# Unit 14's slots each fetched by two gathers with bounded row numbers

## The chip, the cores and the metric

The kernel runs on one core of a Trainium2 chip. The metric is the device time of one execution in microseconds. Before the change it is 949.93 us, the median of three runs (949.86 to 950.06). Engine names are those of the profile: PE is TensorE's matmul, PEld its weight load, DVE is VectorE, ACT ScalarE, POOL GpSimd, SP SyncE.

## What is computed

One layer of a hybrid decoder: windowed and block attention, cross-attention, and a product-key expert retrieval (PEER), for 256 tokens of width 1024 in float32. The change lies in the PEER part alone. It is, cut to its core:

```python
PEER_HEADS, PEER_N_KEYS, PEER_TOPK = 8, 128, 16
PEER_N_EXPERTS = PEER_N_KEYS * PEER_N_KEYS            # 16384 rows in each of u and v

def peer(h, w_q, sub_keys, u, v):
    ...
    sc = jnp.einsum('thpc,pkc->thpk', q, sub_keys)
    v1, i1 = lax.top_k(sc, PEER_TOPK)
    cand = (v1[:, :, 0, :, None] + v1[:, :, 1, None, :]).reshape(T, PEER_HEADS, PEER_TOPK * PEER_TOPK)
    cidx = (i1[:, :, 0, :, None] * PEER_N_KEYS + i1[:, :, 1, None, :]).reshape(...)
    top, pos = lax.top_k(cand, PEER_TOPK)
    experts = jnp.take_along_axis(cidx, pos, axis=-1).reshape(T, PEER_HEADS * PEER_TOPK)
    gates = jax.nn.softmax(top, axis=-1).reshape(T, PEER_HEADS * PEER_TOPK)
    ...
    a = jax.nn.gelu(jnp.einsum('cd,ced->ce', xc, u[ec]), approximate=False)
    y = jnp.einsum('ce,ced->cd', gc * a, v[ec])
```

Each token uses 8 heads x 16 experts, and each expert is a row of u (the dot product) and a row of v (what is added, weighted). The final RMSNorm follows.

## The kernel before

The host lays u and v side by side, so that expert e is one row of 2048 floats (8 KB) of `in_experts`, row numbers 0 to 16383.

**Units and slots.** A unit is one head of one tile of 128 tokens (one token on each partition); there are 16 (`UNITS`), numbered 0 to 15, the first eight for tokens 0 to 127. A unit has 16 slots (`TOPK`). Slot s of a unit is the s-th expert of each of its 128 tokens: 128 rows of 8 KB, 1 MiB, in one buffer of SBUF. There are 16 buffers (`BUFFERS`; their names in the trace are `arena` and `late_ring`), and from unit 5 on slot s always uses the same one, so a gather of slot s of a unit waits for the last use of slot s of the unit before.

**Who does what with a slot.** GpSimd issues its gather (`issue`, L2008): an indirect DMA that takes one row number for each partition from `expert[:, parity, s]`. When it has landed it adds 16 to the semaphore of the buffer, `slot_in[b]`. VectorE waits for this semaphore in `dot` (L1876) and computes the 128 dot products. For each pair of slots (`GROUP` = 2) ScalarE applies the gelu and the gates and writes two diagonal matrices (`weigh`, L1306 to L1321), and PE multiplies them with the v halves of the two rows (`use_pair`, L1020 and L1023, on quarters of the array; `use_group`, L957, in units 0 to 4 and 15) and adds up in PSUM. Its last matmul of a slot adds one to `slot_free`, for which GpSimd waits before it issues into the buffer again.

**The order on GpSimd.** Its queue is one list: units 0 to 4 written out, then `gather_unit` for unit 5, a loop over units 6 to 13, `gather_unit` for units 14 and 15. `gather_unit` waits for `experts_ready` once (the unit's row numbers, which VectorE computes two units ahead between its dot products and leaves in `expert`), and for each slot for `slot_free`. A wait is a wait and an empty instruction (`wait_apart`). The last two slots of unit 15 are fetched as u halves and v halves by four gathers (L2040) from `last_rows`.

**The end.** Unit 15's last eight slots go one by one (L1887, L1057); then VectorE and ScalarE normalise tile 1 and the result is stored.

The semaphore count that stands for the landing of slot (u, s) is `landed_count(u, s)`; it is used by `dot`.

Of the kernel before, what the change touches and what calls it, by code (L numbers as in the profile page):

```python
# [7 lines left out]
ALU = mybir.AluOpType  # L8
# [4 lines left out]
U32 = mybir.dt.uint32  # L13

P = 128
# [10 lines left out]
PEER_HEADS, PEER_KEYS, TOPK = 8, 128, 16  # L26
# [35 lines left out]
UNITS = TILES * PEER_HEADS  # L62
SLOTS = UNITS * TOPK
BUFFERS = 16
# [3 lines left out]
AHEAD = 2  # L68
SOFTMAX_AFTER = 6
QUERIES_FIRST = 3  # L70
GATES_AT_SLOT = 5


def over_slots(unit, first, last):
# [16 lines left out]
QUERY_UNITS = PEER_HEADS - QUERIES_FIRST  # L91
# [186 lines left out]
def build(nc, x_in, mem_in, rel_bias, panels, keys_in, experts, gain_cols, gain_rows, ident_in,  # L278
          onehot_in, mask_in, iota_in, out):
    with ExitStack() as ctx:  # L280
        def sb(name, shape, dt=F32):
            return ctx.enter_context(nc.sbuf_tensor(name, shape, dt))

        def sem(name):
            return ctx.enter_context(nc.semaphore(name))
# [24 lines left out]
        neg_max = sb("neg_max", [P, SOFTMAXES, TILES])  # L310
        row_max = sb("row_max", [P, SOFTMAXES, TILES])
# [23 lines left out]
        expert = sb("expert", [P, AHEAD, TOPK], U32)  # L335
# [7 lines left out]
        diag = sb("diag", [P, DIAGS, P])  # L343
        last_rows_f = sb("last_rows_f", [P, 2, HALVED])
        last_rows = sb("last_rows", [P, 2, HALVED], U32)


        with (nc.sbuf_tensor("arena_below", [P, 5120], F32),
# [45 lines left out]
        def at_buffer(b):  # L394

            return ring[:, b, :] if b < RING else late_ring[:, LATE[b - RING], :]

        def buffer_of(u, s):

            first = isinstance(u, int) and u < QUERY_UNITS  # L400
            return BUFFER_OF_SLOT[u * TOPK + s if first else ALL_FROM + s]

        def slot(u, s):

            return at_buffer(buffer_of(u, s))

        low_half, high_half = slice(0, P // 2), slice(P // 2, P)
        unused_raw = raw[:, (RAW_LOADED.index("qpeer4") + 1) % RAW_RING, :]
        crossed, nothing = unused_raw[:, 0:D], unused_raw[:, D:D + P]
        last_squares = slot(UNITS - 1, 0)[:, 0:D]  # L410
# [2 lines left out]
        def landed_count(u, s):  # L413

            if isinstance(u, int) and u < QUERY_UNITS:
                n = u * TOPK + s
                return 16 * BUFFER_OF_SLOT[:n + 1].count(BUFFER_OF_SLOT[n])
            before = BUFFER_OF_SLOT[:ALL_FROM].count(BUFFER_OF_SLOT[ALL_FROM + s])
            return u * 16 + 16 * (before - QUERY_UNITS + 1)

        def query_rows(h, t):

# [72 lines left out]
        experts_ready = sem("experts_ready")  # L495
# [3 lines left out]
        slot_in = [sem(f"slot_in{i}") for i in range(BUFFERS)]  # L499
        slot_free = sem("slot_free")  # L500
# [5 lines left out]
        crossed_out = sem("crossed_out")  # L506
        crossed_summed = sem("crossed_summed")
        last_rows_step = sem("last_rows_step")
        last_rows_ready = sem("last_rows_ready")
        last_down_in = [sem(f"last_down_in{i}") for i in range(HALVED)]  # L510
        last_dot = sem("last_dot")
# [37 lines left out]
        def wait_apart(eng, semaphore, value):  # L549

            eng.wait_ge(semaphore, value)
            eng.nop(nofuse=True)
# [896 lines left out]
        def _(dve):  # L1449
# [412 lines left out]
            def gate_weights(u):  # L1862

                dve.wait_ge(top_exp_ready, u + 1)
                nc.vector.reciprocal(top_inv[:], top_sum[:]).then_inc(gate_step, 1)
                dve.wait_ge(gate_step, u * 2 + 1)
                if not isinstance(u, int) or u:
                    dve.wait_ge(gate_taken, u)
                nc.vector.tensor_scalar(gate_next, top_exp[:], top_inv[:, 0:1], None, ALU.mult
                                        ).then_inc(gate_step, 1)  # L1870

            def dot(u, t, s):

                dve.wait_ge(slot_in[buffer_of(u, s)], landed_count(u, s))
                row = slot(u, s)[:, 0:D]
                i = nc.vector.tensor_tensor_reduce(row, row, h_rows[:, t, :], 1.0, 0.0, ALU.mult,  # L1876
                                                   ALU.add, dots[:, s:s + 1])
                if isinstance(u, int) and u == UNITS - 1 and s >= SINGLES_FROM:
                    i.then_inc(last_dot, 1)
                elif s % GROUP == GROUP - 1:  # L1880
                    i.then_inc(dots_ready, 1)
# [8 lines left out]
            def use_unit(u, t, routed=True):  # L1890

                for s in range(TOPK):
                    dot(u, t, s)
                    if s == GATES_AT_SLOT:
                        gate_weights(u + 1)
# [72 lines left out]
        def _(pool):  # L1968
# [38 lines left out]
            def issue(u, s, parity):  # L2007
                nc.gpsimd.indirect_dma_start(  # L2008
                    out=slot(u, s), out_offset=None, in_=experts,
                    in_offset=bass.IndirectOffsetOnAxis(ap=expert[:, parity, s:s + 1], axis=0),  # L2010
                ).then_inc(slot_in[buffer_of(u, s)], 16)
# [34 lines left out]
            def gather_unit(u, parity, joins=(), last=TOPK):  # L2046
                pool.wait_ge(experts_ready, u + 1)
                for s in range(last):
                    n = ALL_FROM + s
                    if n in joins:  # L2050
                        pool.wait_ge(product_ready, PLACE[f"qpeer{PEER_HEADS - 1}"] + 1)
                    elif joins and n < min(joins):
                        wait_apart(pool, slot_free, SLOT_BEFORE[n] + 1)
                    else:
                        wait_apart(pool, slot_free, u * TOPK + (s + 1 - BUFFERS))
                    issue(u, s, parity)

            gather_unit(QUERY_UNITS, QUERY_UNITS % AHEAD, [n for n in JOINS if n >= ALL_FROM])
            with pool.Fori(QUERY_UNITS + 1, UNITS - AHEAD, AHEAD) as u:
                for k in range(AHEAD):  # L2060
                    gather_unit(u + k, (QUERY_UNITS + 1 + k) % AHEAD)
            gather_unit(UNITS - 2, UNITS % AHEAD)
            gather_unit(UNITS - 1, (UNITS - 1) % AHEAD, last=TOPK - HALVED)
            pool.wait_ge(last_rows_ready, 1)
            for i in range(HALVED):
                s = TOPK - HALVED + i
# [100 lines left out]
```

## Time and profile before

| | us |
|---|---|
| median of three runs | 949.93 |
| the profiled execution | 950.31 |
| its span on the core | 948.5 |
| DVE busy | 621.1 |
| PE busy | 743.5 |
| POOL busy | 350.1 |
| gathers, issue to landing, median | 30.9 and 30.2 (two tiles) |

The span is what the profile of the program covers; the time of an execution has 1.8 us more around it. The profile divides the span into 40 slices of 23.7 us and gives the busy tenths of each engine in each; its DMA row is the mean busy share of the sixteen DMA engines, the row under it what they moved. The gathers of the experts begin at 292 us. The mean granted clock of TensorE is 0.903.

### The profile page before, as it was taken

What the parts mean: (1) busy time and instruction counts of PE and PEld (TensorE: products, weight loads), DVE (VectorE), ACT (ScalarE), POOL (GpSimd) and SP (SyncE); (2) the same over time, 40 slices, a digit from 0 to 9 for tenths busy, and PEclk for the clock granted to TensorE, in tenths of its full rate; (3) what the DMA queues carried; (4) which work ended last, traced back from release to release, by engine and by line L of the source; (5) the groups of instructions that cost most, each with busy time, mean ns of one, the idle gap of its engine ahead of it and who ended that gap; (6) DMA issues with size and microseconds to landing.
All of it is one profiled execution on the core that took longest, in us unless ns stands there. A gap on an engine that the chain in (4) does not pass through costs nothing.

```text
span 948.5 us, 13013 instructions
## 1 busy us (share of the span) xinstructions
PE 743.5 (78%) x4316; PEld 454.1 (48%) x4316; DVE 621.1 (65%) x1460; ACT 409.2 (43%) x1000; POOL 350.1 (37%) x307
## 2 busy tenths in 40 slices
PE   9999999999988899998897555555555656555676
PEld 7999998799977445564352111111111111111122
DVE  5534685565577886877777666666676766665555
ACT  5544565544574554543533424234232442324242
POOL 1000065050005565665445444534444434343420
PEclk9999999999999999999999787788788687777699
DMA  7897423266328999999999999999999999999995
GB/s 296 247 229 218 168 100 133 89 229 259 135 110 312 423 420 420 421 421 422 421 420 422 421 421 423 422 419 423 423 421 422 422 422 422 422 422 421 422 421 218
DMA packets 49092, 324.90 MB, mean 343 GB/s; under 512 B 5540, under 2 KB 8856, under 8 KB 10648
## 3 DMA queue, kind: packets, MB, share of 16 engines
q0 software_dynamic: 37152, 268.45, 68.1%
q1 hardware_dynamic: 9064, 52.99, 15.7%
q10 hardware_dynamic: 2832, 2.88, 2.1%
q8 instruction: 26, 0.43, 0.2%
q14 instruction: 18, 0.15, 0.0%
HBM read 322.77 MB, written 1.54 MB: 342 GB/s over the span
## 4 chain that ended last, share of the span: by engine, by line
DMA 45%; PE 39%; issue 6%; ACT 6%; DVE 4%; POOL 1%; SPq 0%; ACTq 0%; DVEq 0%; POOLq 0%
DMA arena<-in_experts,expert 37%; PE y L957 8%; PE ps L630 7%; PE ps L632 6%; PE ps L631 6%; DMA late_ring<-in_experts,expert 6%; PE y L1020 3%; DVE w_lo L1464 2%; ACT w_hi L1086 1%; ACT diag L1321 1%; PE ps L771 1%; ACT acts L1314 1%; PE ps L759 1%; POOL late_ring L2008 1%; DMA raw<-in_panels 1%
## 5 line engine op out<-in xcount | busy, mean ns | idle before, releaser
L1020 PE MATMUL y<-late_ring,diag 64*64 64x512 f32 x400 | 138.3, 823 | 106.5 <-ACT diag L1321 106.5
L1876 DVE CUSTOM_DVE_ANT_0 arena<-arena 128x1024 f32<-128x1024 f32 x127 | 155.5, 1224 | 100.5 <-DMA arena<-in_experts,expert 100.2
L2008 POOL DMA_INDIRECT late_ring<-in_experts,expert x127 | 149.4, 1177 | 178.1 <-PE ps L1023 122.5
L1876 DVE CUSTOM_DVE_ANT_0 late_ring<-late_ring,arena 128x1024 f32<-128x1024 f32 x129 | 157.8, 1223 | 83.8 <-DMA late_ring<-in_experts,expert 83.5
L2008 POOL DMA_INDIRECT arena<-in_experts,expert x127 | 149.3, 1176 | 138.1 <-PE ps L1023 72.3
L1306 ACT ACTIVATE acts<-dots 128x2 f32<-128x2 f32 x124 | 25.2, 203 | 319.2 <-DVE dots L1876 319.1
L1023 PE MATMUL ps<-arena,diag 64*64 64x512 f32 x400 | 140.5, 838 | 0.0
L1020 PEld LDWEIGHTS y<-late_ring,diag 64*64 64x64 f32 x400 | 34.9, 167 | 210.0 <-issue 210.0
L1464 DVE TENSOR_TENSOR w_lo<-raw,w_hi 128x2048 fp32r<-128x2048 f32 x38 | 89.5, 2356 | 69.4 <-ACT w_hi L1086 69.4
L1020 PE MATMUL y<-arena,diag 64*64 64x512 f32 x240 | 84.2, 833 | 64.5 <-ACT diag L1321 64.5
L630 PE MATMUL ps<-h_hi,w_hi 128*128 128x256 f32 x384 | 111.5, 290 | 0.0
L632 PE MATMUL ps<-h_hi,w_lo 128*128 128x256 f32 x384 | 108.6, 283 | 0.0
L631 PE MATMUL ps<-h_lo,w_hi 128*128 128x256 f32 x384 | 108.6, 283 | 0.0
L1086 ACT CAST w_hi<-raw 128x2048 fp32r<-128x2048 f32 x39 | 74.3, 1905 | 44.8 <-DMA raw<-in_panels 31.5
L1321 ACT ACTIVATE diag<-ident,acts 128x128 f32<-128x128 f32 x248 | 86.0, 394 | 13.2 <-PE y L957 4.2
L957 PE MATMUL y<-late_ring,diag 128*128 128x512 f32 x180 | 84.2, 607 | 7.0 <-ACT diag L1321 7.0
L957 PE MATMUL y<-arena,diag 128*128 128x512 f32 x172 | 79.1, 597 | 9.8 <-ACT diag L1321 9.8
L1023 PE MATMUL ps<-late_ring,diag 64*64 64x512 f32 x240 | 82.2, 820 | 0.0
L1020 PEld LDWEIGHTS y<-arena,diag 64*64 64x64 f32 x240 | 21.1, 167 | 124.9 <-issue 124.9
L630 PEld LDWEIGHTS ps<-h_hi,w_hi 128*128 128x128 f32 x384 | 73.6, 192 | 3.5 <-issue 3.2
L631 PEld LDWEIGHTS ps<-h_lo,w_hi 128*128 128x128 f32 x384 | 73.6, 192 | 1.2 <-issue 1.2
L632 PEld LDWEIGHTS ps<-h_hi,w_lo 128*128 128x128 f32 x384 | 73.6, 192 | 0.0
(294 smaller groups left out, 1339.1 us busy)
## 6 DMA issues: line engine op xcount, KB each, us to landing
raw<-in_panels SPq DMA_DIRECT2D x40, 1024.0 KB, 4.9
arena<-in_panels SPq DMA_DIRECT2D x6, 1024.0 KB, 6.8
arena<-line_scratch ACTq DMA_DIRECT2D x8, 320.0 KB, 8.2
arena<-in_experts,expert POOLq DMA_INDIRECT x127, 30.9
late_ring<-in_experts,expert POOLq DMA_INDIRECT x127, 30.2
x<-in_x SPq DMA_DIRECT2D x2, 512.0 KB, 3.8
arena<-in_mem SPq DMA_DIRECT2D x1, 1024.0 KB, 8.4
out<-x SPq DMA_DIRECT2D x3, 256.0 KB, 7.0
```

Source lines behind the costliest of these rows:

```text
L630: pe.matmul(dst, stationary[0], moving[0], start=first, stop=False)
L631: pe.matmul(dst, stationary[0], moving[1], start=False, stop=False)
L632: return pe.matmul(dst, stationary[1], moving[0], start=False, stop=last)
L957: mm = pe.matmul(y[:, t, half * 512:(half + 1) * 512], diag[:, s % DIAGS, :], row[:, at:at + 512], start=False, stop=False, skip_group_che ...
L1020: straight = pe.matmul(y[rows, t, cols], diag[rows, a % DIAGS, rows], slot(u, a)[rows, down], start=False, stop=False, skip_group_check=True)
L1023: across = pe.matmul(ps[to, 2 * t + half, :], diag[rows, b % DIAGS, rows], slot(u, b)[rows, down], start=False, stop=False, skip_group_che ...
L1086: nc.scalar.copy(split_parts(n)[0], raw_panel(n)).then_inc(w_hi_ready, 1)
L1306: nc.scalar.activation(acts[:, g * GROUP:(g + 1) * GROUP], dots[:, g * GROUP:(g + 1) * GROUP], ACT.Gelu).then_inc(acts_ready, 1)
L1321: i = nc.scalar.activation(diag[:, s % DIAGS, :], ident[:], ACT.Copy, scale=acts[:, s:s + 1])
L1464: nc.vector.tensor_tensor(low, raw_panel(n), high.bitcast(F32), ALU.subtract).then_inc(w_lo_ready, 1)
L1876: i = nc.vector.tensor_tensor_reduce(row, row, h_rows[:, t, :], 1.0, 0.0, ALU.mult, ALU.add, dots[:, s:s + 1])
L2008: nc.gpsimd.indirect_dma_start(out=slot(u, s), out_offset=None, in_=experts, in_offset=bass.IndirectOffsetOnAxis(ap=expert[:, parity, s:s ...
```

## The change

Unit 14's gathers are replaced by pairs of gathers. For each slot a first gather is issued with the same row numbers and a bound of 8191: a partition whose row number is larger is skipped. A second gather into the same buffer uses another list, `upper`, with a bound of 16383. In that list a row number below 8192 has 16384 added to it, so that it lies over the bound and is skipped. Before the unit GpSimd computes `upper` from `expert` in four operations on 128x16 elements, each waiting for the one before, in the space of two old tiles. The second gather of slot s is issued after the first gather of slot s + 6, and waits until the first gather of slot s has landed. `slot_in` of each buffer then counts 16 more in unit 14; `landed_count` adds them for units 14 and 15. Nothing else is changed.

```diff
+TWICE_UNIT = 14
+UPPER_BEHIND = 6
+LOWER_EXPERTS = PEER_KEYS * PEER_KEYS // 2
...
+        upper = sb("upper", [P, TOPK], U32)
...
+        upper_f = row_max[:].rearrange("p a b -> p (a b)")[:, 0:TOPK]
+        spare_rows = neg_max[:].rearrange("p a b -> p (a b)")[:, 0:TOPK]
...
-            return u * 16 + 16 * (before - QUERY_UNITS + 1)
+            twice = 16 if isinstance(u, int) and u >= TWICE_UNIT else 0
+            return u * 16 + 16 * (before - QUERY_UNITS + 1) + twice
...
+        upper_step = sem("upper_step")
...
+            def issue_within(u, s, rows, last_row):
+
+                nc.gpsimd.indirect_dma_start(
+                    out=slot(u, s), out_offset=None, in_=experts,
+                    in_offset=bass.IndirectOffsetOnAxis(ap=rows[:, s:s + 1], axis=0),
+                    bounds_check=last_row, oob_is_err=False,
+                ).then_inc(slot_in[buffer_of(u, s)], 16)
+
+            def upper_part(u, s):
+                wait_apart(pool, slot_in[buffer_of(u, s)], landed_count(u, s) - 16)
+                issue_within(u, s, upper, 2 * LOWER_EXPERTS - 1)
+
+            def gather_unit_twice(u, parity):
+                pool.wait_ge(experts_ready, u + 1)
+                rows = expert[:, parity, :]
+                nc.gpsimd.tensor_copy(upper_f, rows).then_inc(upper_step, 1)
+                pool.wait_ge(upper_step, 1)
+                nc.gpsimd.tensor_scalar(spare_rows, upper_f, float(LOWER_EXPERTS),
+                                        float(2 * LOWER_EXPERTS), ALU.is_lt, ALU.mult).then_inc(upper_step, 1)
+                pool.wait_ge(upper_step, 2)
+                nc.gpsimd.tensor_tensor(upper_f, upper_f, spare_rows, ALU.add).then_inc(upper_step, 1)
+                pool.wait_ge(upper_step, 3)
+                nc.gpsimd.tensor_copy(upper[:], upper_f).then_inc(upper_step, 1)
+                pool.wait_ge(upper_step, 4)
+                for s in range(TOPK):
+                    wait_apart(pool, slot_free, u * TOPK + (s + 1 - BUFFERS))
+                    issue_within(u, s, rows, LOWER_EXPERTS - 1)
+                    if s >= UPPER_BEHIND:
+                        upper_part(u, s - UPPER_BEHIND)
+                for s in range(TOPK - UPPER_BEHIND, TOPK):
+                    upper_part(u, s)
...
-            gather_unit(UNITS - 2, UNITS % AHEAD)
+            gather_unit_twice(UNITS - 2, UNITS % AHEAD)
```

Below, L3 stands for the first (lower) gather of unit 14's slot 3 and U3 for its second (upper) one.

## Rows read from the trace of the kernel before

**Rows 1.** The page: span, and busy tenths in 40 equal slices of it.
```profile
span 948.5 us, 13013 instructions
...
PE   9999999999988899998897555555555656555676
...
DVE  5534685565577886877777666666676766665555
...
DMA  7897423266328999999999999999999999999995
GB/s 296 247 229 218 168 100 133 89 229 259 135 110 312 423 420 420 421 421 422 421 420 422 421 421 423 422 419 423 423 421 422 422 422 422 422 422 421 422 421 218
```

**Rows 2.** Busy time by stretch, all engines; last come clock, DMA share, GB/s.
```profile
core 0: us, PE busy (x) PEld busy (x) DVE busy (x) ACT busy (x) POOL busy (x), PEclk, DMA share, GB/s
791.00:830.00 39.00, 22.80 (x128) 6.02 (x128) 26.39 (x72) 13.87 (x44) 17.20 (x16) 0.73 1.01 422
830.00:870.00 40.00, 23.16 (x128) 6.07 (x128) 25.67 (x70) 14.97 (x46) 17.20 (x16) 0.70 1.01 422
870.00:910.00 40.00, 24.83 (x130) 6.85 (x127) 20.23 (x35) 12.00 (x42) 18.36 (x18) 0.74 1.01 422
```

**Rows 3.** Chain of waits from 820: start us, length us, what.
```profile
831.64 32.43 DMA arena<-in_experts,expert
...
903.23 32.54 DMA arena<-in_experts,expert
...
937.71 5.63 PE y L1057 x12
```

**Rows 4.** Timeline of VectorE at unit 14's first dot products: start us, us, instruction.
```profile
861.61 1.23 DVE L1876 CUSTOM_DVE_ANT_0 late_ring<-late_ring,arena 128x1024 f32<-128x1024 f32 x1 [0.83 <-DMA late_ring<-in_experts,expert]
...
864.09 1.23 DVE L1876 CUSTOM_DVE_ANT_0 arena<-arena 128x1024 f32<-128x1024 f32 x1 [1.25 <-DMA arena<-in_experts,expert]
```

**Rows 5.** The gathers' line L2008: duration in ns, then time to landing.
```profile
L2008 POOL DMA_INDIRECT arena<-in_experts,expert x127: 939/957/2874, 292.6 to 903.2; - x127
...
DMA to landing us min/median/max: 5.7/30.5/33.8
```

**Rows 6.** Timeline of GpSimd: end of unit 13's gathers and unit 14's first.
```profile
827.93 0.95 POOL L2008 DMA_INDIRECT late_ring<-in_experts,expert  x1 [0.30 <-issue]
830.06 1.28 POOL L2008 DMA_INDIRECT late_ring<-in_experts,expert  x1 [1.18 <-PE ps L1023]
```

**Rows 7.** Timeline of GpSimd: back-to-back gathers of the last unit.
```profile
907.21 0.94 POOL L2040 DMA_INDIRECT late_ring<-in_experts,last_rows  x1 [0.30 <-issue]
908.46 0.95 POOL L2040 DMA_INDIRECT late_ring<-in_experts,last_rows  x1 [0.30 <-issue]
```

**Rows 8.** GpSimd's groups by line: its smallest operation and a small subtraction.
```profile
L2003 POOL TENSOR_TENSOR o_lo<-arena,o_hi 128x256 fp32r<-128x256 f32 x2 | 1.5, 730 | 75.4 <-ACT arena L1248 75.4
...
L1970 POOL MEMSET spare<- 128x1 f32 x1 | 0.1, 98 | 0.3 <-POOLq L2160 0.3
```

**Rows 9.** Timeline of VectorE and GpSimd around the kernel's first gather.
```profile
291.55 0.17 DVE L1824 CAST expert<-expert_f 128x8 uint32<-128x8 f32 x1
...
292.65 1.15 POOL L2008 DMA_INDIRECT arena<-in_experts,expert  x1 [3.09 <-DVE expert L1824]
```

**Rows 10.** The page: DMA queues with packets, MB and share of 16 engines.
```profile
q10 hardware_dynamic: 2832, 2.88, 2.1%
q8 instruction: 26, 0.43, 0.2%
```

**Rows 11.** Timeline of PE: first steps of a pair at either clock.
```profile
882.84 1.12 PE L1020 MATMUL y<-late_ring,diag 64*64 64x512 f32 x2 [1.29 <-ACT diag L1321]
...
883.72 1.09 PE L1020 MATMUL y<-late_ring,diag 64*64 64x512 f32 x2
...
887.81 0.65 PE L1020 MATMUL y<-arena,diag 64*64 64x512 f32 x2 [1.28 <-ACT diag L1321]
...
888.26 0.62 PE L1020 MATMUL y<-arena,diag 64*64 64x512 f32 x2
```

## The prediction

> **What bounds the kernel now.** I read the page's busy rows first [rows 1]. In the last two thirds of the span the row DMA stands at 9 and its GB/s row at 419 to 423, while DVE and PE fall to 5 to 7 tenths: the sixteen DMA engines are the bound of the expert stage. The table by stretches says the same of the part that the change touches [rows 2]: DMA share 1.01 and 421 to 422 GB/s in each of three stretches of 39 or 40 us, with POOL busy 17.2 to 18.4 us and DVE 20 to 26 us. The chain of waits ends with gathers of 32 to 33 us, each from issue to landing, until 935.77, and then with a PE tail of 5.63 us [rows 3]. VectorE's own rows give the beat: dot products of unit 14 start at 861.61 and 864.09, 2.48 us apart, each about 1.25 us idle until its gather has landed [rows 4]. So one slot (1 MiB, 128 rows of 8 KB) costs the DMA engines about 2.49 us, whatever the compute engines do.
>
> What keeps them busy is a queue. A gather takes 30.5 us (median) from issue to landing [rows 5], so some 12 slots stand in it. GpSimd issues unit 14's first gather at 830.06 and the dot product that uses it starts at 861.61 [rows 4, 6]: 31.5 us. It then waits for free buffers, which come in pairs every 5 us. It has slack: a gather costs it 0.94 us and back to back they start 1.25 us apart [rows 7], against a beat of 2.49. The question is whether the queue ever runs dry under the new order.
>
> **The change, part by part.**
>
> *Bytes.* Each of the 2048 rows of unit 14 is still fetched once, by one gather or the other. Worked out from the reference's inputs, 1121 of them are lower and 927 upper, so a half gather is worth about 1.24 us of DMA time. Nothing is saved.
>
> *Four small GpSimd operations before unit 14.* The trace has none of this size on 16 columns; between a 128x1 memset (0.10 us) and a 128x256 subtraction (0.73 us) [rows 8], with 0.3 us between them [rows 7], they cost 4 x 0.4 to 1.03 = 1.6 to 4.1 us. GpSimd is through unit 13 at 828.9 and waits until 830.06 anyway [rows 6], so the first gather slips by 0.5 to 3 us. The 12 slots in front of it hide that: zero at the end.
>
> *The new wait, and what queues behind it.* GpSimd issues L0 to L6 (lower parts) in some 15 us, paced by free buffers, and then stands before U0 until L0 has landed, at about 861. Behind this wait stand L7, every later part of unit 14 and all of unit 15. Meanwhile the DMA engines eat the old queue. When L0 lands, only L1 to L6 are left: 6 x 1.24 = 7.4 us of work instead of 30. From the landing to U0's first byte: a released gather started 0.93 us after the cast that it waited for (cast end 291.72, gather 292.65) [rows 9], and the shortest landing in the trace is 5.7 us [rows 5], which less 2.49 us of data leaves 3.2 for issue, start and receipt. Together at most 4.1 us. Reserve for an average engine: 7.4 - 4.1 = 3.3 us.
>
> *GpSimd becomes as slow as the DMA.* From then on each pair (a lower, an upper part) takes GpSimd 2 x 1.25 = 2.50 us and the DMA 2.49: the reserve neither grows nor shrinks as long as a gather takes 0.94 us. It often doesn't: in 791 to 830 sixteen gathers were busy 17.20 us, 1.075 each [rows 2], 0.13 more, and the long ones begin inside a dot product. In the first 9 us after U0 VectorE has nothing to work on (slot 0 is whole only at about 870), so 7 of the 26 gathers run free and 19 pay: 19 x 0.13 = 2.5 us. Left: 0.8 us.
>
> *The rows don't split evenly over the engines.* A gather leaves eight rows to each of sixteen engines; of the 48 rows of L1 to L6 an engine has 24 on average with a spread of sqrt(48)/2 = 3.5, and the lightest of sixteen some two spreads less, 7 rows or 7 x 2.49/8 = 2.2 us. The lightest engine therefore runs dry for 2.2 - 0.8 = 1.4 us. A lost engine microsecond isn't given back: every engine has eight rows in each slot of unit 15, and a slot is whole only with its last row.
>
> Two sentences on the notes, which the sum doesn't need. The Trainium skill, "DMA: Bandwidth & Descriptors", section "The descriptor swizzle", gives the engine of each partition; by it the reference's indices put 18 of those 48 rows on the lightest engine, 1.9 us, in line with the 2.2. Its section "Anatomy of one DMA — SWDGE (gpsimd) path" fits 2.0 us + bytes / 436e3 to each DMA, which would put 16 x 2.0 = 32 us on sixteen more of them; the trace disagrees for queued ones, since 1 MiB every 2.48 us [rows 4] leaves 0.08 us beside the 2.40 of bytes, not 2.0.
>
> *Skipped rows.* No gather here skips one. Of 256 rows that two gathers name, 128 are skipped, 8 per engine and slot, 128 per engine in all. At best they cost nothing; at worst each is like the small packets of queue 10, 2.1% of 16 x 948.5 us over 2832 packets = 112 ns [rows 10], 14.4 us in all. Those carry 1 KB and a skipped row carries nothing, so I take a value near the lower end, 4 ns: 0.5 us.
>
> *More code.* Queue 8 fetched 0.43 MB of instructions in 26 packets for 13013 executed ones [rows 1, 10]: 33 bytes each, so some 70 more on GpSimd are a seventh of one fetch, and a fetch occupies an engine for 0.2% of 16 x 948.5 / 26 = 1.2 us: 0.2 us.
>
> *VectorE, ScalarE, PE.* Slots 0 to 9 of unit 14 are whole some 7.5 us later, since L0 to L6 go ahead of U0, and slots 10 to 15 then follow at 1.24 us. VectorE does a dot product in 1.23 us, and ScalarE was busy 14.97 us in the stretch with eight pairs, under 1.9 each [rows 2, 4]; PE starts a pair's four steps 0.43 us apart at the full clock (from 887.81) and 0.86 apart at half (from 882.84), 1.7 and 3.4 us for a pair [rows 11], against 2.5 us that a pair then takes to arrive: at half clock, which held in part of these stretches (granted 0.70 to 0.74 [rows 2]), three pairs leave 3 x 0.9 = 2.7 us of backlog. Unit 15's first pair has 5 us, so it is gone long before the tail. Buffers: slot 0 of unit 14 is free by about 878, and GpSimd asks for it only after U15, near 895. Zero, hidden by GpSimd's own lateness.
>
> *Sum.* 1.4 (dry) + 0.5 (skipped rows) + 0.2 (code) = 2.1 us on the chain. The profiled execution took 950.31 us (span 948.5 and 1.8 around it), 0.38 above the median of 949.93; it becomes 952.4, and the median 952.0.
>
> **The rivals.**
>
> 1. *The reserve suffices* (not slower). If U0's data begin within 7.4 - 2.5 - 2.2 = 2.7 us of L0's landing, instead of 4.1, no engine runs dry, and what is left is 0 to 0.8 us: 950.3. The 4.1 is an upper bound (its 3.2 has the landing's receipt and the engines' uneven start in it), which speaks for this. The same outcome follows with 4.1 us if the gathers of these 30 us aren't slowed by dot products.
>
> 2. *A bounded gather costs GpSimd more.* From 0.03 us more per gather (0.8 / 26) the average engine is dry too, and the loss is 26 x extra. At 1.20 us per gather (the one at 830.06 took 1.28 [rows 6]) the pair takes 3.0 us: 26 x 0.25 = 6.5, less the reserve of 3.3, plus 2.2 for the lightest engine: 5.4 us, with skipping and code 6.1: 956.0. The longest gather of the trace took 2.87 us [rows 5]; at 2.2 us it would be 26 x 1.26 - 3.3 = 29.5 us, 979.4. For it: the bound must be looked at for every row. Against: a row that is skipped needs no descriptor, which makes a gather cheaper. The Trainium skill, "GPSIMD Engine Reference", section 3.1, puts data-dependent branching at about 12 cycles per element, which for 128 rows at its 1.2 GHz is an estimate of 1.28 us per gather, that is this case at 2.2 us; no run so far has a branching gather.
>
> 3. *Skipped rows are moved all the same*, only not written. Then unit 14 is 32 slots long: 16 x 2.49 = 39.8 us, 990. Against: the operation is meant to skip.
>
> **How the numbers follow.** A measurement of this kernel can tell about 0.2%, 1.9 us, from no change; the line lies at 951.8, inside my own case. Forecast (the lightest engine dry, 0.8 to 4 us): 0.50. Rival 1: 0.22. Rival 2: 0.24, of it 0.08 above 10 us. Rival 3: 0.03. The last 0.01 goes to mishaps on the fast side. Of the forecast's 0.50 some 0.19 lies under 951.8; with 0.21 of rival 1 that makes 0.40 within 0.2%; 0.02 faster (0.01 of rival 1, the rest unnamed); and 0.58 slower. Range for 8 in 10: from 950.2 (half of rival 1 below) to 959.0 (rival 2's dear third and rival 3 above).
>
> **What would show it.** Right: GpSimd idle some 14 us before its first upper gather, then 26 gathers with starts 1.25 to 1.4 us apart; VectorE's dot product of unit 14's slot 0 at about 870 instead of 861.6, its last six 1.25 us apart; unit 15's slot 0 at 902.5 + 2; a dip of the DMA share of a few hundredths in 865 to 905. Wrong: gathers over 1.1 us with VectorE idle (rival 2), DMA bytes up by 16 MB (rival 3), a share of 1.01 throughout (rival 1). A DMA gap in another place, or an end that moves without unit 15's first dot product moving, would refute the argument itself.

## The result, and the profile after

Time after: 954.84 us, median of 5 runs (952.14 to 957.03), beside 950.06 us (949.86 to 950.56) for five runs of the kernel before on the same chip: a ratio of 1.005, 95% interval 1.0029 to 1.0071, so some 4.8 us slower. The profiled execution took 957.03 us. The source of after has eight lines more ahead of the part in question: L1876 is L1884 here, L1020 is L1028, L2008 is L2016, and the bounded gathers have line L2068.

The page of after, with the lines that answer to [rows 1] and [rows 10]:

```profile
span 955.2 us, 13081 instructions
...
POOL 1000065050004455555445444344444444436850
...
DMA  8797533256337999999999999999999999999996
GB/s 311 223 207 200 189 118 133 89 224 261 133 110 297 423 417 408 421 422 421 421 421 421 422 422 421 422 421 422 421 421 423 421 422 422 423 421 402 328 422 278
DMA packets 51397, 324.92 MB, mean 340 GB/s; under 512 B 7844, under 2 KB 11160, under 8 KB 12952
...
q8 instruction: 26, 0.43, 0.2%
...
HBM read 339.54 MB, written 1.54 MB: 357 GB/s over the span
```

The GB/s row has a hole in slices 37 and 38 (402 and 328 where [rows 1] has 421 and 422), while the DMA row still prints a 9. The same by stretches, to be laid beside [rows 2]; the last three columns are TensorE's granted clock, DMA share and GB/s:

```profile
core 0: us, PE busy (x) PEld busy (x) DVE busy (x) ACT busy (x) POOL busy (x), PEclk, DMA share, GB/s
...
830.00:870.00 40.00, 24.57 (x128) 6.44 (x128) 24.27 (x70) 13.74 (x41) 15.95 (x17) 0.70 1.01 416
870.00:910.00 40.00, 23.43 (x125) 6.60 (x128) 20.80 (x35) 11.11 (x41) 31.90 (x27) 0.60 0.95 359
```

In 870 to 910 GpSimd (POOL) is busy 31.90 us instead of 18.36, and the transfers run at 359 GB/s instead of 422. GpSimd's timeline shows why (to be read beside [rows 6, 7]):

```profile
830.64 0.47 POOL L2081 CAST row_max<-expert 128x16 f32<-128x16 uint32 x1
...
831.87 0.20 POOL L2088 CAST upper<-row_max 128x16 uint32<-128x16 f32 x1
...
847.95 1.36 POOL L2068 DMA_INDIRECT late_ring<-in_experts,expert  x1 [1.12 <-PE ps L1031]
864.24 0.99 POOL L2068 DMA_INDIRECT late_ring<-in_experts,upper  x1 [14.92 <-PE ps L1031]
865.53 0.99 POOL L2068 DMA_INDIRECT late_ring<-in_experts,expert  x1 [0.30 <-issue]
...
896.51 1.93 POOL L2068 DMA_INDIRECT late_ring<-in_experts,upper  x1 [0.30 <-issue]
898.75 1.99 POOL L2068 DMA_INDIRECT late_ring<-in_experts,upper  x1 [0.30 <-issue]
901.04 0.97 POOL L2016 DMA_INDIRECT late_ring<-in_experts,expert  x1 [0.30 <-issue]
```

It stands 14.92 us before the first upper gather. The releaser printed there, PE, had long been done: the wait is for the landing of L0 (wait_only below, with the same wait, prints a landing there). Then 25 gathers (U0 to U15 and L7 to L15) follow back to back until unit 15's first at 901.04: 36.80 us, 1.472 each. VectorE, beside [rows 4]:

```profile
862.16 1.23 DVE L1884 CUSTOM_DVE_ANT_0 late_ring<-late_ring,arena 128x1024 f32<-128x1024 f32 x1 [0.36 <-DMA late_ring<-in_experts,expert]
873.63 1.23 DVE L1884 CUSTOM_DVE_ANT_0 late_ring<-late_ring,arena 128x1024 f32<-128x1024 f32 x1 [9.80 <-DMA late_ring<-in_experts,upper]
...
905.30 1.23 DVE L1884 CUSTOM_DVE_ANT_0 late_ring<-late_ring,arena 128x1024 f32<-128x1024 f32 x1 [0.62 <-DMA late_ring<-in_experts,upper]
909.03 1.23 DVE L1884 CUSTOM_DVE_ANT_0 late_ring<-late_ring,arena 128x1024 f32<-128x1024 f32 x1 [2.49 <-DMA late_ring<-in_experts,expert]
```

These are unit 13's last dot product, unit 14's first and last, and unit 15's first. The chain of waits, beside [rows 3], now has gathers of GpSimd between its DMA pieces:

```profile
838.61 28.04 DMA arena<-in_experts,expert
866.75 0.08 issue
866.83 0.46 POOL arena L2068
...
898.75 6.53 DMA late_ring<-in_experts,upper
905.30 1.23 DVE late_ring L1884
...
918.86 23.59 DMA arena<-in_experts,expert
...
946.39 3.69 PE y L1065 x8
```

A gather that landed 30 us after its issue lands after 6.53 us here: nearly all of the queue in front of it is gone.

**Two measures that I use from here on.** Unit 13's last dot product starts at 859.12 in before and at 862.16 in after: 3.04 of the 6.7 us between the two spans lie ahead of unit 14. So I measure a kernel's *stage* from the start of that dot product to the end of the span: 89.38 us before, 93.04 after, a loss of 3.66. And I count what the gathers' DMA queue moves later than 65.88 us behind that start (925.0 in before): 4.39 MB before, 7.07 MB after. At 422 GB/s the 2.68 MB are 6.4 us by which the *average* DMA engine is behind. That the two numbers differ turns out to matter. The last column is GpSimd's time for the 25 gathers, from the start of U0 to that of unit 15's first gather, where the wait stands six slots behind.

| kernel | stage, us | loss | of it until unit 15's first dot | average engine behind, us | 25 gathers, us |
|---|---|---|---|---|---|
| before | 89.38 | | | | |
| after | 93.04 | 3.7 | 3.5 | 6.4 | 36.80 |
| behind6_again | 94.98 | 5.6 | 5.4 | 7.8 | 38.39 |
| upper_last | 94.85 | 5.5 | 3.2 | 5.6 | 36.02 |
| behind3 | 98.42 | 9.0 | 8.4 | 10.9 | |
| behind9 | 90.48 | 1.1 | 1.0 | 2.8 | |
| behind12 | 90.53 | 1.2 | 2.7 | 2.0 | |
| wait_only | 89.35 | 0.0 | 0.0 | 0.1 | |
| bounded_once | 89.42 | 0.0 | 0.0 | 0.4 | |
| layout_only | 89.38 | 0.0 | 0.0 | -0.2 | |
| columns6 | 90.39 | 1.0 | 0.9 | 2.7 | 32.83 |
| columns6_slower | 95.16 | 5.8 | 4.5 | 7.4 | 37.60 |
| even6 | 91.28 | 1.9 | 0.8 | 4.3 | 34.39 |
| even6_again | 95.58 | 6.2 | 1.4 | 4.4 | 34.48 |

The medians of three sets of runs of this order (after, upper_last, behind6_again) lie 4.8, 4.8 and 5.0 us over the kernel before; their stages lost 3.7, 5.5 and 5.6. So the whole loss lies in the stage, and the profiled execution of after was the mildest of the three there.

### The profile page after: what moved, and what is told of

Read it like the earlier page. It is cut to its first block, busy times and chain, and to the rows that moved or that the text cites. A ratio compares the mean times of both kernels' runs of the same rounds, so it can differ in the third digit from the quotient of the medians.

```text
span 955.2 us, 13081 instructions
## 1 busy us (share of the span) xinstructions
PE 749.8 (78%) x4316; PEld 455.6 (48%) x4316; DVE 620.8 (65%) x1460; ACT 409.0 (43%) x1000; POOL 362.3 (38%) x327
## 2 busy tenths in 40 slices
DMA packets 51397, 324.92 MB, mean 340 GB/s; under 512 B 7844, under 2 KB 11160, under 8 KB 12952
## 3 DMA queue, kind: packets, MB, share of 16 engines
HBM read 339.54 MB, written 1.54 MB: 357 GB/s over the span
## 4 chain that ended last, share of the span: by engine, by line
DMA 46%; PE 31%; issue 7%; ACT 7%; DVE 6%; POOL 3%; POOLq 0%; ACTq 0%; DVEq 0%; SPq 0%
DMA arena<-in_experts,expert 34%; PE y L965 8%; DMA raw<-in_panels 6%; DMA late_ring<-in_experts,expert 5%; PE ps L638 4%; PE ps L640 4%; PE ps L639 4%; DVE w_lo L1472 3%; PE y L1028 3%; ACT w_hi L1094 3%; ACT diag L1329 1%; PE ps L779 1%; POOL arena L2068 1%; ACT acts L1322 1%; POOL late_ring L2016 1%
## 5 line engine op out<-in xcount | busy, mean ns | idle before, releaser
L1028 PE MATMUL y<-late_ring,diag 64*64 64x512 f32 x400 | 143.9, 852 | 110.7 <-ACT diag L1329 110.7
L1884 DVE CUSTOM_DVE_ANT_0 arena<-arena 128x1024 f32<-128x1024 f32 x127 | 155.6, 1226 | 97.6 <-DMA arena<-in_experts,expert 89.4
L1884 DVE CUSTOM_DVE_ANT_0 late_ring<-late_ring,arena 128x1024 f32<-128x1024 f32 x129 | 157.8, 1224 | 87.9 <-DMA late_ring<-in_experts,expert 72.6
L2016 POOL DMA_INDIRECT late_ring<-in_experts,expert x119 | 132.5, 1113 | 161.2 <-PE ps L1031 99.3
L2016 POOL DMA_INDIRECT arena<-in_experts,expert x119 | 138.9, 1167 | 123.5 <-PE ps L1031 59.9
L1031 PE MATMUL ps<-arena,diag 64*64 64x512 f32 x400 | 144.8, 862 | 0.0
L1028 PEld LDWEIGHTS y<-late_ring,diag 64*64 64x64 f32 x400 | 35.6, 171 | 215.2 <-issue 215.1
L1028 PE MATMUL y<-arena,diag 64*64 64x512 f32 x240 | 84.9, 841 | 57.3 <-ACT diag L1329 57.3
L1031 PE MATMUL ps<-late_ring,diag 64*64 64x512 f32 x240 | 84.3, 838 | 0.0
L1028 PEld LDWEIGHTS y<-arena,diag 64*64 64x64 f32 x240 | 21.5, 171 | 121.0 <-issue 121.0
```

The lines of the kernel that those rows point to most:

```text
L1028: straight = pe.matmul(y[rows, t, cols], diag[rows, a % DIAGS, rows], slot(u, a)[rows, down], start=False, stop=False, skip_group_check=True)
L1031: across = pe.matmul(ps[to, 2 * t + half, :], diag[rows, b % DIAGS, rows], slot(u, b)[rows, down], start=False, stop=False, skip_group_che ...
L2016: nc.gpsimd.indirect_dma_start(out=slot(u, s), out_offset=None, in_=experts, in_offset=bass.IndirectOffsetOnAxis(ap=expert[:, parity, s:s ...
```

## The experiments

The theories by letter: D is the forecast's own, that the wait empties the DMA queue and GpSimd can't refill it. L says that part of the loss comes from where the new tile `upper` lies in memory, ahead of other tiles; N, that the 3.04 us ahead of the stage are only what one execution differs from another. In the diffs "before" or "after" says which kernel was edited.

**The first 3 us: layout_only (before) and upper_last (after).**

```diff
# layout_only
+        upper = sb("upper", [P, TOPK], U32)
# upper_last: the same line moved behind that of the tile arena
```

> The kernel before with one thing of the change: the tile upper (64 bytes on each partition) is declared in front of arena and never used. In the changed kernel's profile 3.0 us of the 6.7 us more of span lie ahead of unit 14 (unit 13's last dot product at 862.16 instead of 859.12), in the first 100 us, where ScalarE waits 51.2 instead of 31.5 us for the weight panels. Theory L (the shifted tiles slow the early loads): median 952 to 953, spread of some us between executions. Rival N (the early stage merely varies from execution to execution, or depends on the program's code): 949.9 to 950.3, spread under 1 us.

> The changed kernel, with the tile upper declared behind arena, so that arena and all before it lie where they lay in the kernel before. Theory L: the early 3 us go away and only the 3.5 us of units 14 and 15 are left: 953.5, spread under 1 us. Rival N: as the changed kernel, 952 to 957. From unit 13's last dot product to unit 15's first: 46.9 us by both (43.4 before).

layout_only: 950.83 us (949.8 to 953.86, 12 runs) beside 950.72 (947.44 to 953.59, 26 runs), ratio 1.0004 (0.9992 to 1.0017), stage 89.38. upper_last: 955.51 us (951.32 to 959.54, 9 runs), ratio 1.0053 (1.0036 to 1.0069). The tile's place costs nothing and moving it back gives nothing: L falls. The kernel before alone spread over 6 us on that chip, which is N; and behind6_again, the same program as after, has unit 13's last dot product at 858.02 instead of 862.16.

**The wait alone: wait_only (before).** Unit 14 keeps its whole gathers, but GpSimd stands after each until the one six slots ahead of it has landed.

```diff
+                    issue(u, s, parity)
+                    if s >= 6:
+                        wait_apart(pool, slot_in[buffer_of(u, s - 6)], landed_count(u, s - 6))
```

> The kernel before; in unit 14 GpSimd waits, after the gather of slot s + 6, until the gather of slot s has landed (s = 0 to 9). Whole rows, one gather each, nothing skipped. Theory D: the queue then holds 6 whole slots, 14.9 us, when GpSimd is released, and a released gather needs at most 4.1 us: nothing runs dry, from unit 13's last dot product to the end of the span 89.4 us as in the kernel before (89.38), though GpSimd idles some 15 us. Rival W (the wait itself costs): 2 to 4 us more.

951.12 us, one run, stage 89.35. Its GpSimd stands as long as after's does:

```profile
863.23 1.25 POOL L2008 DMA_INDIRECT late_ring<-in_experts,expert  x1 [14.81 <-DMA late_ring<-in_experts,expert]
```

and the transfers don't notice, in the stretches of the same kernel:

```profile
870.00:910.00 40.00, 23.68 (x132) 6.41 (x125) 20.05 (x34) 12.00 (x42) 24.75 (x24) 0.81 1.01 422
```

Six whole slots are 6 x 2.49 = 15 us of work in the queue, and each further gather brings 2.49 us of work for some 1.3 us of GpSimd's (24.75 us for 24 of them in that stretch, and 0.30 behind each). So neither the idle time nor the landing's way back to GpSimd costs anything in itself.

**The bound alone: bounded_once (before).** Unit 14's sixteen whole gathers get a bound that no row exceeds.

```diff
+                        bounds_check=PEER_KEYS * PEER_KEYS - 1, oob_is_err=False,
```

> The kernel before, with unit 14's sixteen gathers given the bound 16383, under which nothing is skipped. If the 0.99 us of a bounded gather on GpSimd (0.94 without) is the price of looking at the bound: 0.99 here too. If it is the price of skipping: 0.94. Unit 13's last to unit 15's first dot product 43.4 us either way, no change of the time.

952.69 us, one run, stage 89.42. The line of these gathers:

```profile
L2066 POOLq MOVE  x16: 29/29/38, 831.7 to 867.0; - x16
L2066 POOL DMA_INDIRECT late_ring<-in_experts,expert x8: 995/1002/1359, 832.5 to 868.8; - x8
```

0.995 us at least instead of 0.939 [rows 5], and a 29 ns MOVE in GpSimd's sequencer that fits into the 0.30 us between two gathers. A bounded gather that skips half its rows took the same (0.99). So the bound costs 0.05 us, and skipping costs GpSimd nothing.

**The distance: behind3, behind9, behind12 and behind6_again (after).** The last is the same program as after, as a second sample.

```diff
-UPPER_BEHIND = 6
+UPPER_BEHIND = 12
```

> The changed kernel with the upper gathers twelve slots behind instead of six. The reserve when the first lower part lands is then 12 x 1.24 = 14.9 us instead of 7.4, more than GpSimd loses in 26 gathers (26 x (1.42 - 1.24) = 4.7) and in the first start (4.1). Theory D (of the 3.5 us some 2.4 are engines that ran dry, 1.2 are 9 ns for each skipped row): from unit 13's last to unit 15's first dot product 44.6 us, DMA share 1.01 throughout. Rival S (skipped rows cost all of it, as much as 27 ns each): 46.9 as with six. The whole time is 952 to 956, since the early stage is that of the changed kernel.

> The changed kernel with the upper gathers three slots behind instead of six. The queue holds 3 x 1.24 = 3.7 us at the first release instead of 7.4. Theory D: 3.7 us more dry time than with six: from unit 13's last dot product to the end 96.5 to 98.5 (89.4 before, 93.0 and 94.9 with six, 90.5 with twelve). Rival (the loss comes from the gathers themselves, wherever they stand): 93 to 95.

> The changed kernel once more (the same program), beside behind9. Its loss from unit 13's last dot product to the end was 3.7 and 5.5 us over 89.4 in two executions: again 93 to 95, if these are what the order costs and their difference is how GpSimd's gathers happen to meet VectorE's dot products; nearer to 91.5 if both earlier ones were accidents.

> The changed kernel with the upper gathers nine slots behind. At the first release the queue holds 9 x 1.24 = 11.2 us. Theory D: the dry time is gone or nearly so, since three slots more are 3.7 us and the dry time with six was 2.5 to 4.3: from unit 13's last dot product to the end 90.5 to 91.3 (90.53 with twelve, 98.42 with three). Rival (a loss that falls evenly with the distance, 98.4, 93 to 95, 90.5): 92 to 92.5.

behind3: 958.83 us, one run. behind6_again: 955.18 (4 runs), ratio 1.006 (1.0043 to 1.0078). behind9: 952.57 (10 runs), 1.0021 (1.0004 to 1.0038). behind12: 951.91 (10 runs), 1.0013 (1.0001 to 1.0024). The stage's loss goes 9.0, then 3.7 to 5.6, then 1.1 and 1.2 with distances 3, 6, 9, 12: it falls as the queue at the wait grows, and stops falling. behind12's stretches, of 24 us each:

```profile
860.00:884.00 24.00, 3.91 (x20) 0.90 (x16) 1.74 (x8) 2.28 (x6) 17.07 (x17) 0.57 1.02 409
884.00:908.00 24.00, 16.73 (x127) 5.10 (x128) 20.04 (x36) 11.77 (x45) 19.25 (x12) 0.83 1.02 411
```

The share never falls, but GB/s stands at 409 to 411. (Its first dot product of unit 15 is 2.7 us late, where the expectation had 1.2: VectorE takes unit 14's in one heap, 1.15 us apart, which theory D had left out. Unit 15 makes that good.) That floor of some 1.1 us is what the doubled gathers cost the DMA engines, whatever the wait does. Each engine has 128 skipped rows, so it is some 9 ns for each; the trace agrees, in which the 1335 packets under 512 B of behind12's 862 to 885 took 9 ns each (median). The average engine is 2.0 us behind in behind12, 0.8 more than the stage. The page of after says what a skipped row is: 2304 packets more than before, all under 512 B (7844 to 5540), which is 2048 skipped rows and 16 small packets for each of the sixteen further gathers; the bytes moved are the same, 324.92 and 324.90 MB. The page's figure for HBM reads rises all the same, from 322.77 to 339.54 MB, by 2048 x 8 KB.

**The split: columns6 and even6 (after).** columns6 fetches the first half (4 KB) of every row and, six slots behind, the second half, with the same waits and as many gathers, but no bound and nothing skipped. even6 keeps bound and skipping but puts the even partitions into the first gather and the odd ones into the second, through row numbers beyond the bound, so that each half has 64 rows. In both, the four small operations on GpSimd compute the new row numbers (what they need in even6, VectorE prepares once, ahead of unit 5).

```diff
# columns6
-                    out=slot(u, s), out_offset=None, in_=experts,
+                    out=slot(u, s)[:, last_row * D:(last_row + 1) * D], out_offset=None,
+                    in_=experts.rearrange("e (h d) -> (e h) d", h=2),
...
-                    bounds_check=last_row, oob_is_err=False,
...
# even6
...
-                    issue_within(u, s, rows, LOWER_EXPERTS - 1)
+                    issue_within(u, s, rows, 2 * LOWER_EXPERTS - 1)
```

> The changed kernel, but the first gather fetches the u halves of all 128 rows (4 KB each) and the second the v halves: the same order, wait and number of gathers, no bound, no skipped row, each engine eight half rows in each. A gather costs GpSimd 0.94 instead of 0.99 us. From unit 13's last dot product to the end: 1.0 us for twice 4 KB at 159 ns instead of once 8 KB at 309 to 313, 0.1 for the counters, nothing dry: 90.5. If the dry time came from something else than uneven rows and the 0.05 us: 92 or more.

> The changed kernel, but the first gather takes the rows of the even partitions and the second those of the odd ones, so that each engine has four rows in each. Still 32 gathers, 2048 skipped rows, six behind, the same wait. From unit 13's last dot product to the end: 89.4 before, 93.0 and 94.9 in two executions of the changed kernel, 90.5 with the upper gathers twelve behind. If the uneven split over the engines makes part of the dry time: 90.5 for the skipped rows plus 0 to 1 = 90.5 to 91.5. If the dry time is the mean queue running out, split evenly or not: 93 to 95.

> The kernel with even partitions first and odd ones six behind once more (the same program). From unit 13's last dot product to the end it took 91.28 us, against 93.0, 94.9 and 95.0 in three executions of the lower/upper split and 89.4 before. If the even split over the engines is worth 2 us or more: 90.5 to 92 again, and a whole time 2 to 3 us over the kernel before. If the one execution was luck: 93 to 95 and 4.5 to 5 us over.

columns6: 951.33 us (10 runs), ratio 1.0016 (1.0006 to 1.0025), loss 1.0 us. Its stretches:

```profile
860.00:884.00 24.00, 9.14 (x48) 2.38 (x48) 7.86 (x17) 5.12 (x17) 17.46 (x18) 0.72 1.02 402
884.00:908.00 24.00, 16.17 (x104) 5.12 (x104) 15.39 (x28) 9.17 (x35) 17.70 (x18) 0.86 1.01 402
```

The same wait at the same distance, and most of the loss is gone. GpSimd needed 1.275 us for each of the first 24 gathers here, and stood 0.97 us longer than usual for the landing of L15 before the last; in after a gather took 1.472.

even6: 952.72 us (5 runs), ratio 1.0033 (1.0014 to 1.0053). The same program again, even6_again: 954.96 us (6 runs), 1.0042 (1.0029 to 1.0055), with a stage of 95.58, above both of its expected ranges. Until unit 15's first dot product both lose 0.8 and 1.4 us, less than any of the three executions split by expert (3.2 to 5.4). Behind it even6_again loses 4.8 us more, in another way. One line of ScalarE:

```profile
902.73 0.69 ACT L1331 ACTIVATE diag<-ident,acts 128x128 f32<-128x128 f32 x2 [8.54 <-remote]
```

and its chain of waits:

```profile
894.19 8.46 another core or an unknown queue
...
927.85 7.06 PE y L967 x16
934.91 13.75 PE y L1067 x32
948.66 0.02 issue
```

ScalarE stood 8.5 us on something that the trace can't name; PE, which had little to do meanwhile (3.69 us in 890 to 900) and a granted clock of 0.55 there, near the lower level of 1.2 GHz, got its work in a heap and then bound the tail: the chain is PE from 903.57 on. upper_last ends in the same way, with a piece of 5.81 us of unknown origin and the same 13.75 us of PE. What ScalarE waited for stays open.

Nor do the two runs show that even rows are cheaper for the DMA engines, because GpSimd's time changed along with the rows: its 25 gathers took 34.39 and 34.48 us, with two long ones each, against 36.02 to 38.39 when split by expert. In all seven executions of the last column the average engine is behind by that time less 30.1 to 30.6 us: 30.1 in even6 and even6_again, 30.4 to 30.6 in the three split by expert, 30.1 and 30.2 in columns6 and columns6_slower. The slowest engine, which decides when a slot is whole, shows the same: unit 15's first dot product is late by GpSimd's time less 32.8 to 33.3 us when split by expert, and less 33.1 and 33.6 in the two even ones. So some 0.4 us is left for the rows themselves, no more than executions of one order differ by. What differs too is VectorE's beat, 2.5 to 2.6 us between unit 14's first dot products in even6 and 2.2 to 2.9 in after. The even rows may help by that way, through fewer gathers that meet a dot product; no run separates it.

**Less pace: columns6_slower (columns6).** A memset with a wait ahead of every second later half takes some of GpSimd's time away.

```diff
+                if s % 2 == 0:
+                    nc.gpsimd.memset(qpT[:, 0, 0, :], 1.0).then_inc(upper_step, 1)
+                    pool.wait_ge(upper_step, 5 + s // 2)
```

> The kernel with u halves first and v halves six behind, and on GpSimd a memset of 128x256 with a wait for it ahead of every second v gather: 0.31 us, and a gather behind a waited operation starts 0.9 us later instead of 0.3, so 8 x 0.9 = 7.2 us more for GpSimd in the unit. DMA work is unchanged. Without it 90.39 from unit 13's last dot product to the end. Theory D: the reserve at the first release is 6 x 1.27 = 7.6 us, of which 2.7 to 4.1 go before the first byte, so 3.5 to 4.9 us are free and the loss is 7.2 less these: 92.7 to 94.1. If GpSimd's pace doesn't set the loss: 90.4. If each of its microseconds counts in full: 97.6.

955.73 us, one run, stage 95.16: a miss, by over 1 us. Three of GpSimd's lines:

```profile
869.89 1.94 POOL L2068 DMA_INDIRECT arena<-in_experts,expert  x1 [0.30 <-issue]
871.83 0.33 POOL L2077 MEMSET qpT<- 128x256 f32 x1
872.42 1.93 POOL L2068 DMA_INDIRECT late_ring<-in_experts,upper  x1 [0.27 <-POOL qpT L2077]
```

The memsets cost some 0.3 us each, but they also shift the gathers against VectorE's beat, and four of them took 1.9 us. The 25 gathers took 37.60 us instead of 32.83: 4.8 more. Unit 15's last dot product comes 4.5 us later than in columns6, and the average engine is 4.6 us further behind; the 0.2 us more in the stage are PE's, whose 13.75 us end the chain here too. So nearly each microsecond of GpSimd's counted, and next to no reserve was left in columns6; D had granted it several microseconds.

## Why the prediction was right or wrong

The time lies in the range, and the kernel is slower by more than 0.2%, the case that I gave 0.58. The main mechanism, a queue emptied by the wait that GpSimd can't refill, is the forecast's. The size is not: 2.1 us was the sum, 4.8 was measured. That it is not further off is partly luck: reserve, interference and bound were each set too kindly, by some 5.5 us together, and the uneven rows and the engine that ends last too harshly, by nearly as much. Point by point:

- **The bound now, and the wait.** Right. GpSimd's idle time was 14.92 us (some 14 forecast), and slot 0's dot product came 11.47 us after unit 13's last instead of 2.49, so 9.0 us later than before (8.4 forecast). That the wait costs nothing but through the queue is shown by wait_only.
- **The reserve of 3.3 us.** Wrong. It was 7.4 us of queue less 4.1 for the way back. By the line through the seven executions (the average engine behind by GpSimd's time less 30.1 to 30.6 us), the 2.0 us of behind12, whose queue stays deep, are reached when the 25 gathers take some 32.3 us. That is 1 us over 25 x 1.25: an estimate of the reserve from these runs. columns6 fits it: it has no bound and even halves, its first 24 gathers took 30.60 us (0.6 over 24 x 1.25), and its average engine is 2.7 us behind all the same. columns6_slower shows that GpSimd's further time counts nearly in full. I had read the way back from one gather's landing time, and I took L1 to L6 as whole when L0 landed. A slot has landed when its slowest engine has delivered, and by then the others may have eaten into the next ones (below); that this is the missing part is my reading, and no run shows it apart.
- **GpSimd's pace.** Right in kind, too small twice over. I counted 26 gathers where there are 25. Interference was 36.80 - 25 x 1.295 = 4.4 us, where 2.5 was forecast, and 6.0 and 3.6 in behind6_again and upper_last. And the 1.295 itself is 0.05 above the 1.25 of [rows 7]: the bound costs 25 x 0.05 = 1.3 us, which the forecast set at nothing and only rival 2 had. That rival's point of decision was 0.03 us per gather, and 0.05 is beyond it, so its mechanism is there, at a fifth of its smaller price (0.25 us) and a twenty-fifth of its larger one (1.26). The Trainium skill, "GPSIMD Engine Reference", section 3.1, by which branching per element gives an estimate of 1.28 us per gather, does not carry over to this bound: bounded_once shows 0.05.
- **The sum with these terms.** 1.0 of reserve less 4.4 and 1.3 leaves the average engine dry for 4.7 us; with the 2.0 of behind12 it is 6.7 us behind, where 6.4 was measured.
- **"A lost engine microsecond isn't given back."** Wrong. In after the average engine is 6.4 us behind, the stage only 3.7. In behind3, behind9, columns6, columns6_slower, behind6_again and even6 the stage's loss is also 1.6 to 2.4 us below the average engine's, in behind12 0.8; in upper_last and even6_again PE ended the stage. The GB/s of before in 930 to 950, in steps of 0.5 us, show what gives it back:

```profile
GB/s 418 393 393 426 393 434 418 393 361 352 287 197 74 74 66 49 33 25 25 33 8 0 0 0 0 0 0 0 0 0 0 0 213 385 373 78 0 0 0 0
```

  and of after, in the same stretch:

```profile
GB/s 455 381 422 422 442 393 463 426 442 393 459 426 393 459 410 410 426 426 426 410 401 418 377 410 426 401 410 418 401 410 401 254 131 57 0 0 0 0 0 0
```

  Before, the rate has halved by 935.5 and a thin remainder goes on until past 940, from 74 down to 25 GB/s, where one of sixteen engines has 26 of the 422: I read this as engines staggered by some 5 us, of which only the last one sets the end. After, the full rate holds until 945.5 and all is over by 947. By this reading the first two microseconds or so that an average engine loses come out of that stagger. Two errors thus worked against each other: the queue was reckoned too well filled, and the end was hung on every engine instead of the last one.
- **Uneven rows.** The step that the sum's 1.4 us rest on, a lightest engine with 2.2 us less work than the average, isn't borne out. even6's first dot product of unit 15 comes 0.8 and 1.4 us late, against 3.2, 3.5 and 5.4 split by expert, but GpSimd's shorter time explains all but some 0.4 us of that. In after it was the average engine that ran dry, by GpSimd's pace.
- **Skipped rows.** 9 ns each instead of 4: 1.1 us instead of 0.5, far below the upper end of 112 ns. Rival 2's argument that a skipped row needs no descriptor and makes a gather cheaper fails: it leaves a packet, and the gather takes 0.99 us either way. That queued gathers don't pay the 2.0 us each of the Trainium skill's fit per DMA in "DMA: Bandwidth & Descriptors", section "Anatomy of one DMA — SWDGE (gpsimd) path", is shown again: sixteen more of them and 2048 skipped rows cost 1.1 and 1.2 us together in behind9 and behind12.
- **Code: 0.2 us.** Nothing seen: 26 packets in queue 8 as before, and 19 instead of 18 in the other instruction queue, 14. The four small operations took from 830.64 to 832.07, 1.4 us, and are hidden.
- **PE: zero, hidden.** Right in after, wrong as a rule. In three of the profiled executions, upper_last, columns6_slower and even6_again, PE bound the tail: from unit 15's last dot product to the end it is 9.95, 9.40 and 13.08 us there, and 9.1 to 9.3 in the others. That is 0.8, 0.2 and 3.9 us of loss, in each with a piece that the trace can't name ahead of it in the chain.
- **Rival 1** (the reserve suffices) falls with the result. **Rival 3** (skipped rows are moved) falls by the 324.92 MB. Who had looked at the HBM figure alone, with its 16.8 MB more, would have taken rival 3 for true; the time and the moved bytes say otherwise.
- **What would show it.** The dip was called "a few hundredths" of the DMA share. It was 0.06 in 870 to 910, but 63 of 422 GB/s: the share hardly falls where the rate does, and GB/s is the better witness. The gathers' starts were 1.29 to 2.29 us apart and not 1.25 to 1.4, unit 14's last six dot products 1.15 to 2.42 us apart and not 1.25, and unit 15's first came 3.5 us later and not 2.

No version beats the kernel before. behind12, columns6 and behind9 come closest and are 0.1 to 0.2% behind it, since every one has sixteen gathers more and none saves a byte.

## What to carry to other kernels

A wait inside the engine that feeds a DMA queue is free only while the work left in the queue at its release covers the way to the next byte and everything by which the feeder is slower afterwards: wait_only, with 2.49 us of work per gather, paid nothing, and after, with 1.24 us of work for 1.3 us of feeding at best and 1.5 on average, paid 4.8. Count that work per DMA engine, for the one that ends last, not for the average, and don't reckon with a reserve made of two estimates when the feeder's pace equals the queue's. When two kernels differ in their loss, lay the feeder's own time beside it first: here it explains all but some 0.4 us of a gain that looked like one of evener rows. Splitting a transfer in two halves the work that each instruction of the feeder buys, and that alone can make the feeder the bound.

## What the runs showed of the hardware

- A bound on an indirect gather of 128 rows costs GpSimd 0.05 us (0.99 to 0.94), skipping or not, and one 29 ns MOVE. Each skipped row still leaves a packet under 512 B, some 9 ns of an engine's time, and the HBM read figure rises by 8 KB for it though the moved bytes don't.
- A gather that begins while VectorE is in a dot product can take twice its time: 1.85 to 1.99 us in after, 1.9 in columns6_slower. In after, behind the wait, such a gather ends 0.86 to 0.88 us behind the end of the dot product: those at 881.21, 884.66, 889.05 and 898.75 lasted 1.85, 1.23, 1.86 and 1.99 us, beside dot products of 1.23 us from 880.97, 883.80, 888.81 and 898.65. Without a bound it is 0.81 to 0.83 (in before 1.36 us from 859.80, with a dot product from 859.12). Those that begin in the last 0.1 us of one take their usual time. So the price, up to 1 us, depends on how the two engines' beats fall: those of columns6 that met a dot product mostly began 0.2 us before its end and took 0.95 to 1.02 us, and a 0.3 us memset in between brings four long ones.
- The sixteen DMA engines, each with eight rows of every slot, don't end together in the kernel before: their common rate falls off over some 6 us.
- The same program differs by 4 us from one profiled execution to another ahead of the changed part (unit 13's last dot product at 862.16 in after, at 858.02 in behind6_again), so a comparison of two profiles has to be made from an event inside the stage.
